# When tile 2's expert rows are fetched back from DRAM: after the last pair's weights, with the pooling weights scaled earlier

## The reference, cut to what matters

```
x   = layer_norm(ALPHA * x + mixer(x))
ffn = routed_experts(x) + shared_expert(x)
x   = layer_norm(ALPHA * x + ffn)
```

## Time and profile before

| | us |
|---|---|
| median of 3 runs (1353.47 to 1354.51) | 1353.63 |
| the profiled execution's own time | 1357.86 |
| its span | 1355.9 |
| PE busy in the span | 1286.8 (95%) |
| DMA, mean over the span | 329 GB/s |

### The profile page before, as it was taken

The page is one execution under the profiler, slowest core; times in us unless marked ns, Lnnn a source line. Parts: engine busy times, 40 slices in busy tenths (PEclk is TensorE's granted clock), DMA queues, the critical chain, the costliest instruction groups (busy, mean ns, idle before and its releaser), DMA issues.

```text
span 1355.9 us, 17911 instructions
## 1 busy us (share of the span) xinstructions
PE 1286.8 (95%) x6318; PEld 649.6 (48%) x6318; DVE 570.4 (42%) x1229; ACT 337.4 (25%) x689; POOL 274.7 (20%) x240
## 2 busy tenths in 40 slices
PE   6999988999999999999999789999999999999985
PEld 4566546545444454444533665544444444454432
DVE  0665546433333333323342784332333333343336
ACT  0642412222222222222211341222222212222113
POOL 6130101122211221111221201121112211221120
PEclk9999898999999999999998879999999999999988
DMA  8533028599999999999999723999999999999992
GB/s 276 131 131 125 10 101 324 205 378 411 417 385 420 420 390 422 419 420 392 419 324 399 324 94 128 377 402 411 389 420 420 420 393 419 420 389 420 364 375 81
DMA packets 81940, 446.22 MB, mean 329 GB/s; under 512 B 20754, under 2 KB 22914, under 8 KB 31648
## 3 DMA queue, kind: packets, MB, share of 16 engines
q1 hardware_dynamic: 69248, 428.13, 78.7%
q0 software_dynamic: 12640, 17.39, 4.5%
HBM read 436.37 MB, written 35.31 MB: 348 GB/s over the span
## 4 chain that ended last, share of the span: by engine, by line
PE 89%; DMA 5%; DVE 3%; ACT 1%; issue 1%; SPq 0%; DVEq 0%
PE bank L981 32%; PE bank L900 20%; PE bank L934 15%; PE bank L928 9%; DMA sb_wslot<-in_moe_w_up_dram 4%; PE bank L884 3%; PE bank L1323 3%; PE bank L1109 1%; PE bank L1072 1%; PE bank L993 1%; DMA sb_x<-in_x_sample_dram 1%; PE bank L1100 0%; PE bank L1402 0%; ACT sb_xt L1510 0%; PE bank L1240 0%
## 5 line engine op out<-in xcount | busy, mean ns | idle before, releaser
L756 POOL TENSOR_TENSOR sb_sent<-sb_yh,sb_yl 128x1024 f32<-128x1024 f32 x56 | 134.2, 2397 | 705.7 <-DVE sb_yl L1735 579.5
L981 PE MATMUL bank<-sb_wslot,sb_xt 128*64 128x512 f32 x1024 | 232.7, 608 | 11.3 <-DMA sb_wslot<-in_moe_w_up_dram 11.3
L934 PE MATMUL bank<-sb_wslot,sb_ht 128*64 128x512 f32 x1024 | 231.0, 593 | 0.0
L981 PE MATMUL bank<-sb_wslot,sb_xg_own 128*64 128x512 f32 x1024 | 226.5, 595 | 1.7 <-ACT sb_xg_own L1454 1.7
L1729 DVE TENSOR_TENSOR sb_x<-sb_x,bank 128x512 f32<-128x512 f32 (+1 forms) x284 | 175.6, 681 | 80.3 <-PE bank L928 80.1
L1754 DVE TENSOR_TENSOR sb_hh<-sb_sg,bank 128x256 f32<-128x256 f32 x64 | 27.0, 422 | 397.3 <-ACT sb_sg L1479 397.3
L1735 DVE SCALAR_TENSOR_TENSOR sb_yl<-bank,sb_gslot,sb_yh 128x512 fp32r<-128x512 f32 x128 | 96.1, 751 | 160.6 <-ACT sb_yh L1461 160.6
L1479 ACT ACTIVATE sb_sg<-bank 128x256 f32<-128x256 f32 x64 | 24.6, 384 | 532.8 <-PE bank L981 532.8
L981 PEld LDWEIGHTS bank<-sb_wslot,sb_xt 128*64 128x64 f32 x1024 | 71.9, 139 | 155.6 <-issue 155.6
L900 PE MATMUL bank<-sb_pick,sb_xh 128*128 128x512 f32 x384 | 144.2, 405 | 0.0
L934 PEld LDWEIGHTS bank<-sb_wslot,sb_ht 128*64 128x64 f32 x1024 | 72.7, 137 | 144.6 <-issue 140.7
(11 more groups left out here) (326 smaller groups left out, 1157.8 us busy)
## 6 DMA issues: line engine op xcount, KB each, us to landing
sb_wslot<-in_moe_w_gate_dram SPq DMA_DIRECT2D x64, 2048.0 KB, 10.4
sb_wslot<-in_moe_w_up_dram SPq DMA_DIRECT2D x64, 2048.0 KB, 15.4
sb_wslot<-in_moe_w_down_dram SPq DMA_DIRECT2D x64, 2048.0 KB, 17.5
sb_w_in_hi<-in_w_in_dram SPq DMA_DIRECT2D x2, 2048.0 KB, 14.8
tail_slots<-sb_sq POOLq DMA_DIRECT2D x16, 256.0 KB, 4.5
sb_w_in_lo<-in_w_out_dram SPq DMA_DIRECT2D x1, 4096.0 KB, 14.0
sb_w_in_lo<-in_w_in_dram SPq DMA_DIRECT2D x2, 1024.0 KB, 11.6
sb_ln_g<-in_ln_g_dram POOLq DMA_DIRECT2D x4, 512.0 KB, 4.9
```

What stands on the lines that cost most here:

```text
L756: gp.tensor_tensor(sent[:, :], yh[:, :].bitcast(F32), yl[:, :].bitcast(F32), ALU.add).then_inc(s["sent_made"], 1)
L934: last = pe.matmul(y_b[c][64 * e:64 * e + 64, :], ht[:, k, 64 * e:64 * e + 64], w_down[slot(l, u)][:, e, k * D + c * 512:k * D + (c + 1) * ...
L981: last = pe.matmul(gu_b[64 * e:64 * e + 64, :], xgt[b][:, k, sl], w_gu[slot(l, u)][:, :, e, k * FE:(k + 1) * FE], start=k == 0, stop=k == ...
```

## The change

POOL's readback of `tail_slots` waits for the last down weights of slot 1 in both layers (`down_in1`). SP's wait before the router's and shared weights is now for the last scatter (`all_sent`) and no longer for the first tail step. DVE no longer waits for the tail before the six end sums; POOL's last add waits for all six, and ACT's moments and DVE's norm of tile 2 wait for that add. DVE scales `pool_w` between layer 0's norms of tile 1 and tile 2 instead of after them.

```diff
@@ semaphores
-            "y_summed", "tail_sent", "slot_free", "sent_made", "tail_in", "tail_step")} for l in range(DEPTH)]
+            "y_summed", "tail_sent", "slot_free", "sent_made", "all_sent", "tail_in", "tail_step")} for l in range(DEPTH)]
@@ sp_experts
-                sp.wait_ge(s["tail_step"], 1)
+                sp.wait_ge(s["all_sent"], 1)
                 sp.wait_ge(s["down_done0"], uses)
                 load_shared(sp, 1)
@@ pool_experts
             src = slots.rearrange("(t k) d -> t (k d)", k=TOPK)
+            gp.sem_inc(s["all_sent"], 1)
+            gp.wait_ge(s["down_in1"], rounds * (16 * TURNS))
+            gp.sem_inc(s["all_sent"], 1)
             for h in range(2):
                 for r0, n in ((0, TAIL), (SAMPLE_ROW, N_DEC)):
                     gp.dma_start(xg_own[64 * h + r0:64 * h + r0 + n, :], src[r0:r0 + n, h * 4096:(h + 1) * 4096]).then_inc(s["tail_in"], 16)
...
-            gp.wait_ge(s["added"], rounds * ROUND_ADDS + 1)
+            gp.wait_ge(s["added"], rounds * ROUND_ADDS + FILLS + 1)
             gp.tensor_tensor(x[0:64, 2, :], x[0:64, 2, :], xg_own[0:64, 0:1024], ALU.add).then_inc(s["tail_step"], 1)
@@ moments (ACT)
-                    act.wait_ge(s["added"], rounds * ROUND_ADDS + TILES + t + 2)
+                    if t == 2:
+                        act.wait_ge(s["tail_step"], 4)
+                    else:
+                        act.wait_ge(s["added"], rounds * ROUND_ADDS + TILES + t + 2)
@@ dve_experts, after the loop
-            dve.wait_ge(s["tail_step"], 4)
             add_sums(rounds * ROUND_ADDS, END_SUM_BANKS, True)
@@ DVE, before layer_norm(2)
-                    dve.wait_ge(s["pool_in"], 16 * 3)
-                    for k in range(2):
-                        dve.tensor_tensor(pool_w[:, :, k, :], pool_w[:, :, k, :], pool_s.rearrange("p (g n) -> p g n", g=4), ALU.mult)\
-                           .then_inc(s["pool_scaled"], 1)
@@ DVE, after the experts
-                layer_norm(2 * l + 1, lambda t, rows: None)
+                def tail_next(t, rows):
+                    if t == 2 and l == 0:
+                        dve.wait_ge(L[1]["pool_in"], 16 * 3)
+                        for k in range(2):
+                            dve.tensor_tensor(pool_w[:, :, k, :], pool_w[:, :, k, :], pool_s.rearrange("p (g n) -> p g n", g=4), ALU.mult)\
+                               .then_inc(L[1]["pool_scaled"], 1)
+                    if t == 2:
+                        dve.wait_ge(s["tail_step"], 4)
+
+                layer_norm(2 * l + 1, tail_next)
```

## The result

Predicted 1350.1 us (1343.5 to 1357.5). Measured: 1360.09 us as the median of five runs (1357.36 to 1361.96), the kernel before beside it 1354.16 us (1353.47 to 1356.69). The ratio is 1.0051 with an interval of 1.0029 to 1.0072: slower by 0.5%, outside the range.

A forecast was written before the change was run, and what follows sets the result against it. PE, busy for 95% of the span, was taken as the bound. Layer 1's -3.5 us and layer 0's 0.0 gave -3.5 on the 1353.6 us median: 1350.1 us, range 1343.5 to 1357.5.

The forecast's parts named there:

- The stalls: PE's idling and clock loss at the 31st pair would go: -8.6 us in layer 0, -8.5 us in layer 1.
- When the readback starts: POOL's readback, after the last down weights land, would start at 729.0 us in layer 0 and 1316.5 in layer 1.
- How long it takes: Readback from first issue to first add: 12.4 us in layer 0, 10.9 us in layer 1, at 218 GB/s.
- Then let pass little of q1: In layer 0, q1's small packets would hardly slow the readback on q0, hence 12.4 us, near layer 1's value.
- (a): Rival: apart from big packets the readback runs at full rate, 7.4 us in both layers, hence 1341.6 us; chance 0.15.
- The tail in layer 0: Last add at 760.9 us, bank copies held up, po at half clock, mx2 ending at 779.8: 0.0 us net.
- each us later moves my time by one: Sign: the first L775, the readback's wait, should start near 741 and 1327 us; each us later adds one.
- The price of the held-up copies: Layer 0: po begins at 766.6 us, its first 5 us at half clock; 10.7 + 2.5 us until mx2 ends.
- The tail in layer 1: Last add at 1343.8 us, span end at 1352.4: 3.5 us earlier, of 8.5 that the loop won.
- (b): Rival: layer 0's readback shares with equals, takes 19.6 us as before, costing +7.2 us, hence 1357.3 us; chance 0.18.
- (c): Rival: DVE and POOL hinder each other, 1.6 us in layer 1, hence 1351.7 us; chance 0.21.
- (d): Rival: the up weights are late by themselves, stalls stay and tails come on top, up to 1365 us; chance 0.04.

The follow-up runs named there:

- e5: Changed kernel, but SP issues the pool_scale broadcast, and the router's, shared and next-pair loads behind it, only after the readback's first add: 1358.3 us, ratio 1.0041.
- e16: Changed kernel with DRAM slots ordered by half and the readback, in its new place, as one contiguous DMA over 128 partitions: 1347.1 us, ratio 0.9958.
- e18: Changed kernel with DRAM slots ordered by half and the readback, in its new place, as two contiguous DMAs of 64 partitions: 1358.7 us, ratio 1.0040.
- e4: Changed kernel, but POOL's readback waits for the last pair's gate and up weights instead of its down weights: 1352.6 us, ratio 0.9994.
- e13: Changed kernel, readback as one DMA over 128 partitions with strided source, layer 0's tile 2 moments behind ScalarE's bank copies: 1435.6 us, ratio 1.0624.

## Why the prediction was wrong

- **The stalls.** Right: the 31st pairs start without idle time and at full clock.
- **When the readback starts.** Right within 0.5 us in both layers.
- **How long it takes: the step that failed.** The prediction had 12.4 us in layer 0 and 10.9 in layer 1; 17.55 and 11.9 were measured. Both rest on 218 GB/s as the readback's own rate. But that is the rate of a mix, in the earlier trace rows, half of it full-width weight packets. In layer 1, alone, the readback moved its 1.57 MB in the chain's 10.28 us, 153 GB/s. That layer 1 was missed by 1.0 us only is luck: the packets moved from 0.9 us after the issue on, where the prediction had 3.7, and then took 11.0 us to the first add instead of 7.2. In layer 0 the start was as forecast (3.9 us), and the rest took 13.7 us instead of 8.7. "Then let pass little of q1" is what failed there besides the rate: the broadcast and the preloads together cost 2.7 us by e5. The prediction rightly put the low rate down to the readback's form, against rival (a), and that is what e16 and e18 show; it missed that the form's own rate lies below that of the mix.

  The Trainium skill has a reason in "SBUF — State Buffer", section "Door 1: The DMA port swizzle": partitions 0 to 63 lie behind eight of 16 ports, and 16 of them behind four. The trace agrees in size, 437 GB/s for 128 partitions alone in layer 1 of e16, and 2.1 MB between 1322 and 1332 us, some 210 GB/s, for 64 in e18; which port was busy no run shows.
- **The tail in layer 0.** Its first adds took 0.9 us more than forecast, the second transfer as before. From a last add 5.5 us late, `mx2` ends 5.3 us later than before: "each us later moves my time by one" held. The price of the held-up copies was right (13.48 us for 13.2).
- **The tail in layer 1.** The second transfer alone took 2.9 us, not 4.4; the readback 1.0 us more; the last two adds 1.1 us more. Then the span ends 5.05 us after VectorE's last instruction instead of 3.0. Together 1355.4 - 0.53 = 1354.9 for 1352.4: of the 3.5 us of gain 1.0 was left. Where the 2 us at the very end come from was not tested. Runs with layer 1's readback in the old place end 3.0 us after that instruction, those with it in the new place 3.6 to 5.1 us (e4 3.0, e13 3.2).
- **The sum.** 5.3 us in layer 0 and 2.5 in layer 1 add 7.8 us to the forecast: 1357.9 instead of 1350.1. The kernel before was 0.5 us slower beside this run than in the prediction's median; 1.7 us up to 1360.1 are left to the spread.
- **Rivals.** (b) had the right place and a part of the cause; its price, 1357.3 for 19.6 us, counted no loss in layer 1. (c) is real too, below, at about 1 us in each layer. (a) and (d) fell: the readback was slow in the absence of big packets as well, and the stalls went.

## What to carry to other kernels

Before moving a transfer out of the way of others, ask why it is in their way. Here a readback over 16 or 32 partitions per DMA halved the total rate while it ran beside the weights (218 GB/s for 419); moved behind the loop it was nearly as slow in layer 0 (17.6 us for 19.6), and now on the path. Given all 128 partitions and contiguous rows, with a third more bytes, it was best left where it stood: 1.2% faster than before, where the move alone was 0.5% slower. And a rate read from mixed traffic is not the rate of one of its parts.

## What the runs showed of the hardware

- **Partitions per DMA** set the rate: 2.1 MB took 8.1 us from issue to first add with one DMA over 128 partitions, 12.7 us with two over 64 (layer 1 of e16 and e18, nothing else under way). In layer 1 of e16 the slices at full rate show 437 GB/s (1308 to 1320 us in 40 slices):

```profile
GB/s 0 0 0 0 0 0 0 765 55 0 164 218 273 437 437 437 437 437 437 437 437 437 437 382 437 219 109 0 0 0 0 0 0 0 0 0 0 0 0 0
```

- **A first dimension of 2** in a DMA's source held 2.1 MB to 53 GB/s, with the 16 engines busy to 0.13, some two of them (e13).
- **VectorE and GpSimd hold each other up.** VectorE's norm instructions with two SBUF inputs take 1.28 us alone and 3.0 to 3.2 us beside GpSimd's adds, whose own 2.34 us grow to 3.10 (VectorE's timeline of the changed kernel, layer 0, then layer 1; GpSimd's rows are above):

```profile
743.77 3.02 DVE L1822 SCALAR_TENSOR_TENSOR sb_x<-sb_x,sb_ln_mv,sb_ln_g 128x1024 f32<-128x1024 f32 x1
...
747.02 3.05 DVE L1826 SCALAR_TENSOR_TENSOR sb_x<-sb_x,sb_ln_rs,sb_ln_b 128x1024 f32<-128x1024 f32 x1
750.10 1.28 DVE L1811 SCALAR_TENSOR_TENSOR sb_x<-sb_x,sb_ln_mv,sb_ln_g 128x1024 f32<-128x1024 f32 x1
...
1339.19 3.24 DVE L1811 SCALAR_TENSOR_TENSOR sb_x<-sb_x,sb_ln_mv,sb_ln_g 128x1024 f32<-128x1024 f32 x1
...
1342.67 3.05 DVE L1814 SCALAR_TENSOR_TENSOR sb_x<-sb_x,sb_ln_rs,sb_ln_b 128x1024 f32<-128x1024 f32 x1
```

The ends fit a lock held for whole instructions: L1822 ends 1.1 us after GpSimd's first add does (741.19 + 4.52 in the chain above). The Trainium skill states such a lock in "SBUF — State Buffer", section "Who interferes with whom", and the trace agrees. It delays whichever comes second. In layer 1 only GpSimd's delay stood on the path: its last two adds took 2.56 and 3.10 us where they took 2.34 and 2.36 before.
